# Attention stage of a hybrid block: modulation product in four column groups, a new spread of the maxima, first scores begun early

## The reference, cut to what matters

```python
def one_block(qi):
    s = jnp.einsum('bqhgd,bkhd->bhgqk', qi.astype(F32), k.astype(F32))
    p = jax.nn.softmax(s, axis=-1)
    return jnp.einsum('bhgqk,bkhd->bqhgd', p, v.astype(F32))
...
mod = jax.nn.silu(cond) @ ada_w + ada_b          # 2 condition rows, 1024 x 6144 weights
```

## Time and profile before

| | us |
|---|---|
| median of 3 runs | 3956.98 |
| the profiled execution | 3956.98 |
| its span | 3955.5 |
| around the span | 1.5 |
| attention stage, about | 357 to 1291 |

### The profile page before, as it was taken

One profiled execution on the slowest core, in us unless ns is written; L12 is line 12 of the kernel. 1 busy time (PEld: TensorE's weight loads), 2 busy tenths in 40 slices (PEclk: granted clock), 3 DMA queues, 4 the chain that ended last, 5 costly groups with the idle time before them and its releaser, 6 DMA issues. The chain is left out here.

```text
span 3955.5 us, 51421 instructions
## 1 busy us (share of the span) xinstructions
PE 3598.2 (91%) x17154; PEld 2926.8 (74%) x17154; DVE 1975.2 (50%) x2945; ACT 1587.8 (40%) x2216; POOL 1050.2 (27%) x606
## 2 busy tenths in 40 slices
PE   5886999999998799787869979999999999999998
PEld 2674666666666799666758768888888888888897
DVE  2765888888886211144753333334334333433364
ACT  2443787777887211265223422222222222222233
POOL 0553888888887000011211100000000000000000
PEclk8997999999999899766989989999999999999999
DMA  4332111110110322133544553334334333533374
GB/s 164 105 111 81 38 42 43 39 42 18 43 42 19 120 81 81 61 97 97 157 153 163 170 164 99 113 98 148 97 112 145 98 102 101 154 95 101 101 207 149
DMA packets 374897, 400.59 MB, mean 101 GB/s; under 512 B 37236, under 2 KB 282196, under 8 KB 374772
## 3 DMA queue, kind: packets, MB, share of 16 engines
q1 hardware_dynamic: 358568, 358.26, 29.2%
q0 software_dynamic: 8432, 31.46, 2.1%
q10 hardware_dynamic: 7776, 9.44, 0.7%
HBM read 318.02 MB, written 81.08 MB: 101 GB/s over the span
## 5 line engine op out<-in xcount | busy, mean ns | idle before, releaser
L796 POOL TENSOR_TENSOR att_tlo<-att_prob,att_thi 128x1024 fp32r<-128x1024 f32 x292 | 694.6, 2397 | 152.1 <-ACT att_thi L963 152.1
L331 PE MATMUL ff_p<-ff_hhi,ff_whi 128*128 128x512 f32 (+1 forms) x1760 | 651.2, 370 | 34.3 <-DVE ff_hlo L2038 22.8
L1982 ACT ACTIVATE ff_whi<-ff_ws 128x2048 fp32r<-128x2048 f32 (+1 forms) x170 | 317.5, 1868 | 902.9 <-PE ff_p L333 885.1
L332 PE MATMUL ff_p<-ff_hlo,ff_whi 128*128 128x512 f32 (+1 forms) x1760 | 650.3, 369 | 0.0
L333 PE MATMUL ff_p<-ff_hhi,ff_wlo 128*128 128x512 f32 (+1 forms) x1760 | 650.3, 369 | 0.0
L1986 DVE TENSOR_TENSOR ff_wlo<-ff_ws,ff_whi 128x2048 fp32r<-128x2048 f32 (+1 forms) x170 | 378.4, 2226 | 386.7 <-ACT ff_whi L1982 386.4
L1928 POOL TENSOR_TENSOR ff_rs<-ff_ms,neg_half 128x1 f32<-128x1 f32 x18 | 9.9, 553 | 1595.1 <-DVE ff_ms L2058 1595.1
L331 PEld LDWEIGHTS ff_p<-ff_hhi,ff_whi 128*128 128x128 f32 x1760 | 334.2, 190 | 91.8 <-issue 36.7
L958 ACT ACTIVATE att_prob<-att_p_s 128x512 f32<-128x512 f32 x584 | 338.3, 595 | 151.3 <-PE att_p_s L856 127.1
L1002 DVE TENSOR_REDUCE att_mx<-att_p_r 128x1 f32<-128x512 f32 x512 | 343.4, 683 | 76.2 <-PE att_p_r L820 76.2
L333 PEld LDWEIGHTS ff_p<-ff_hhi,ff_wlo 128*128 128x128 f32 x1760 | 334.3, 190 | 55.3
(11 more groups left out here) (239 smaller groups left out, 6264.3 us busy)
## 6 DMA issues: line engine op xcount, KB each, us to landing
ff_ws<-in_w_ffn_dram SPq DMA_DIRECT2D x320, 512.0 KB, 4.8
att_aw<-in_ada_w_dram SPq DMA_DIRECT2D x8, 2048.0 KB, 8.3
proj_d<-gp_out SPq DMA_DIRECT2D x18, 784.0 KB, 4.0
hT_d<-qkv_hT SPq DMA_DIRECT2D x18, 512.0 KB, 2.8
qT_d<-qkv_qT SPq DMA_DIRECT2D x18, 512.0 KB, 2.9
att_qa<-qT_d SPq DMA_DIRECT2D x36, 256.0 KB, 2.8
gp_h<-hT_d SPq DMA_DIRECT2D x18, 512.0 KB, 4.9
qkT_d<-gs_qkT SPq DMA_DIRECT2D x18, 512.0 KB, 3.6
```

The costliest lines, as they stand in the source:

```text
L331: pe.matmul(out, ah, bh, start=first, stop=False)
L332: pe.matmul(out, ah, bl, start=False, stop=False)
L796: pool.tensor_tensor(tlo[:, sl, :], prob[:, sl, :], thi[:, sl, :].bitcast(F32), ALU.subtract).then_inc(s.lo, 1)
L1982: act.activation(whi[:, par, 0:cols], ws[:, par, 0:cols], ACT.Copy).then_inc(s.w_hi, 1)
```

## The change

1. `PLAN` becomes 3, 3, 2, 2, 2, 2, 2, 2, 0: the same 18 pieces, more of them in steps 0 and 1, fewer in 3 and 5.
2. The modulation product of a half chunk is made in one step (step 5, at its end) and in four column groups: the two condition rows are padded to 32 stationary columns (`cpad`, made once at the start of the stage), and four products of 64 columns go to the output partitions 0, 32, 64 and 96. That is 8 x 4 matmuls of 64 columns in place of 8 of 256, in one visit in place of four. The bias addition moves to step 6, on 128 partitions x 64; the bias load and the store take the new layout (4 partitions per condition row, two stores in place of one), and SyncE waits for `cpad` before it loads the first chunk.
3. In step 0 of a latent unit, the high parts of both first scores are begun at once, and only their low parts wait for the copy of the maxima; these now stand after the first piece, one behind the other.

```diff
@@ -589,7 +589,7 @@
     FULL = T_LAT // ROW
     N_PIECES = G4 * FULL + G4 // 2
 
-    PLAN = [2, 2, 2, 3, 2, 3, 2, 2, 0]
+    PLAN = [3, 3, 2, 2, 2, 2, 2, 2, 0]
     FOLDED = (2, 6)
     BANKS = 3
     ADDS = 2 * NS - len(FOLDED)
@@ -597,15 +597,17 @@
 
     CHUNKS = N_MOD * D_MODEL // 512 - MOD_FIRST
     HALF = 256
-    CHUNK_STEP = 4
+    CHUNK_STEP = 5
+    COLS = P // 4
+    QUART = HALF // 4
     L_UNITS = 2 * N_LAT
     U_UNITS = 2 * NT
     with ExitStack() as stack:
         ph = Phase(nc, stack, "att")
         s = ph.s
...
         s.q, s.out = [s.q0, s.q1, s.q2, s.q3], [s.out0, s.out1]
         ckr = ph.sb("ckr", [P, 2, KVH, HD])
         cvr = ph.sb("cvr", [P, 2, KVH, HD])
@@ -626,8 +628,9 @@
         osum = ph.sb("osum", [P, 2, P])
         oo = ph.sb("oo", [P, 2, 2 * P])
         aw = ph.sb("aw", [P, KC, 512])
-        adab = ph.sb("adab", [2, 512])
-        mod = ph.sb("mod", [2, 512])
+        cpad = ph.sb("cpad", [P, KC, COLS])
+        adab = ph.sb("adab", [P, 2, QUART])
+        mod = ph.sb("mod", [P, 2, QUART])
         ada_w = g.ada_w.rearrange("l (k p) n -> p (l k) n", p=P)
         p_s = [ph.ps(f"p_s{i}") for i in range(BANKS)]
         p_r = [ph.ps("p_r0"), ph.ps("p_r1")]
@@ -760,8 +763,9 @@
                     cols = bass.ds(c * 512 + MOD_FIRST * 512, 512)
                     sp.dma_start(aw[:, :, :], ada_w[:, :, cols]).then_inc(s.aw, 16)
                     for r in range(2):
-                        sp.dma_start(adab[r:r + 1, :], g.ada_b[:, cols]).then_inc(s.adab, 16)
-
+                        sp.dma_start(adab[r:P:COLS, :, :], g.ada_b[:, cols].rearrange("o (h q n) -> (o q) h n", h=2, q=4)).then_inc(s.adab, 16)
+
+                sp.wait_ge(s.cpad, 1)
                 load_chunk(0)
 
                 def step(S):
@@ -773,13 +777,15 @@
                     if S.after is not None and S.after[1] == 1:
                         c = S.after[0]
                         sp.wait_ge(s.mod, c * 2 + 2)
-                        sp.dma_start(g.mod_d[:, bass.ds(c * 512 + MOD_FIRST * 512, 512)], mod[:, :]).then_inc(s.mout, 16)
+                        for r in range(2):
+                            sp.dma_start(g.mod_d[r:r + 1, bass.ds(c * 512 + MOD_FIRST * 512, 512)].rearrange("o (h q n) -> (o q) h n", h=2, q=4),
+                                         mod[r:P:COLS, :, :]).then_inc(s.mout, 16)
                         if not (isinstance(c, int) and c == CHUNKS - 1):
-                            sp.wait_ge(s.mout, c * 16 + 16)
+                            sp.wait_ge(s.mout, c * 32 + 32)
                             load_chunk(c + 1)
 
                 schedule(sp, step)
-                sp.wait_ge(s.mout, 16 * CHUNKS)
+                sp.wait_ge(s.mout, 32 * CHUNKS)
 
             @block.gpsimd
             def _(pool):
@@ -843,17 +849,21 @@
                         turn(*S.turn)
                     pieces = list(S.max)
 
-                    def scores(i):
+                    def key_cols(e, j, i):
+                        return slice((e.kt0 + 2 * j + i) * P, (e.kt0 + 2 * j + i + 1) * P)
+
+                    def scores_high(i):
                         e, j = S.now
-                        half = (e.g0 + j) * 2 + i
+                        if j == 0 and i == 0:
+                            pe.wait_ge(s.q[e.q], e.q_round * 32 + 32)
+                        wait(pe, s.ex, (e.g0 + j) * 2 + i - (BANKS - 1))
+                        pe.matmul(bank_of(e, j, i)[:, :], g.keysT[:, e.kv, 0, key_cols(e, j, i)], qa[:, e.q, :], start=True, stop=False)
+
+                    def scores_rest(i):
+                        e, j = S.now
                         if j == 0 and i == 0:
                             pe.wait_ge(s.aux, e.n + 1)
-                            pe.wait_ge(s.q[e.q], e.q_round * 32 + 32)
-                        wait(pe, s.ex, half - (BANKS - 1))
-                        bank = bank_of(e, j, i)
-                        kt = slice((e.kt0 + 2 * j + i) * P, (e.kt0 + 2 * j + i + 1) * P)
-                        pe.matmul(bank[:, :], g.keysT[:, e.kv, 0, kt], qa[:, e.q, :], start=True, stop=False)
-                        pe.matmul(bank[:, :], g.keysT[:, e.kv, 1, kt], qb[:, e.q, :], start=False, stop=True).then_inc(s.st, 1)
+                        pe.matmul(bank_of(e, j, i)[:, :], g.keysT[:, e.kv, 1, key_cols(e, j, i)], qb[:, e.q, :], start=False, stop=True).then_inc(s.st, 1)
 
                     def values(i):
                         b, j = S.val
@@ -871,8 +881,13 @@
                         if i == 1:
                             last.then_inc(s.pv, 1)
 
+                    first = bool(late and S.now[1] == 0)
                     if S.now:
-                        scores(0)
+                        scores_high(0)
+                        if first:
+                            scores_high(1)
+                        else:
+                            scores_rest(0)
                     if S.turn and late:
                         turn(*S.turn)
                     if S.turn_sums:
@@ -893,24 +908,30 @@
                         values(0)
                     if pieces:
                         piece(*pieces.pop(0))
-                    if S.now:
-                        scores(1)
+                    if first:
+                        scores_rest(0)
+                        scores_rest(1)
+                    elif S.now:
+                        scores_high(1)
+                        scores_rest(1)
                     if len(pieces) > 1:
                         piece(*pieces.pop(0))
                     if S.val:
                         values(1)
                     for p in pieces:
                         piece(*p)
-                    if S.chunk is not None and CHUNK_STEP <= S.now[1] < CHUNK_STEP + KC // 2:
+                    if S.chunk is not None and S.now[1] == CHUNK_STEP:
 
                         (e, j), (c, half) = S.now, S.chunk
-                        if j == CHUNK_STEP:
-                            wait(pe, s.osum, e.n)
-                            pe.wait_ge(s.aw, c * 16 + 16)
-                        for k in range(2 * (j - CHUNK_STEP), 2 * (j - CHUNK_STEP) + 2):
-                            last = pe.matmul(p_o[1 - e.kv][0:2, 0:HALF], g.cT[:, k::KC], aw[:, k, half * HALF:(half + 1) * HALF], start=k == 0, stop=k == KC - 1)
-                        if j == CHUNK_STEP + KC // 2 - 1:
-                            last.then_inc(s.chunk, 1)
+                        wait(pe, s.osum, e.n)
+                        pe.wait_ge(s.aw, c * 16 + 16)
+                        pe.wait_ge(s.cpad, 1)
+                        for k in range(KC):
+                            for q in range(4):
+                                col = half * HALF + q * QUART
+                                last = pe.matmul(p_o[1 - e.kv][q * COLS:(q + 1) * COLS, 0:QUART], cpad[:, k, :], aw[:, k, col:col + QUART],
+                                                 start=k == 0, stop=k == KC - 1)
+                        last.then_inc(s.chunk, 1)
 
                 schedule(pe, step)
 
@@ -974,6 +995,10 @@
             @block.vector
             def _(dve):
                 dve.memset(ones[:, :], 1.0)
+                dve.memset(adab[:, :, :], 0.0)
+                dve.memset(cpad[:, :, :], 0.0).then_inc(s.zero, 1)
+                dve.wait_ge(s.zero, 1)
+                dve.tensor_copy(cpad[:, :, 0:2], g.cT[:, :].rearrange("p (c k) -> p k c", c=2)).then_inc(s.cpad, 1)
                 dve.memset(wm[:, :, :, :].bitcast(F32), 0.0).then_inc(s.zero, 1)
                 for t in range(2):
                     constant_parts(dve, ckp[:, t])
@@ -990,7 +1015,7 @@
                     dve.tensor_tensor(v_here[:, :, HD:2 * HD], cvr[:, t], v_here[:, :, 0:HD].bitcast(F32), ALU.subtract)
                     last = dve.tensor_tensor(ckp[:, t, :, 2, :], ckr[:, t], ckp[:, t, :, 0, :].bitcast(F32), ALU.subtract)
                 last.then_inc(s.ckl, 1)
-                dve.wait_ge(s.zero, 1)
+                dve.wait_ge(s.zero, 2)
 
                 def piece(v, i, item):
                     bank = item[0]
@@ -1061,12 +1086,11 @@
                                 piece(*pieces.pop(0))
                     for p in pieces:
                         piece(*p)
-                    if S.chunk is not None and S.now[1] == CHUNK_STEP + KC // 2:
+                    if S.chunk is not None and S.now[1] == CHUNK_STEP + 1:
                         e, (c, half) = S.now[0], S.chunk
-                        cols = slice(half * HALF, (half + 1) * HALF)
                         dve.wait_ge(s.chunk, c * 2 + (half + 1))
                         dve.wait_ge(s.adab, c * 32 + 32)
-                        dve.tensor_tensor(mod[:, cols], p_o[1 - e.kv][0:2, 0:HALF], adab[:, cols], ALU.add).then_inc(s.mod, 1)
+                        dve.tensor_tensor(mod[:, half, :], p_o[1 - e.kv][:, 0:QUART], adab[:, half, :], ALU.add).then_inc(s.mod, 1)
 
                 schedule(dve, step)
```

(4 more changed lines are left out.)

## The result

The changed kernel takes 3976.89 us in the median (3974.11 to 3981.11), the kernel before beside it 3957.98 us; ratio 1.0048, 95% interval 1.0035 to 1.0061. It is slower by 19 us, where the forecast was 8.6 us faster. The profiled execution took 3974.11 us, span 3972.2.

A forecast was written before the change was run, and what follows sets the result against it. TensorE was taken to bound product units, GpSimd's chain the second half of plain ones; 16 product units x (0.6 - 1.7) = -17.6 and 15 plain x 0.6 = +9.0 took 3957.0 to 3948.4 us, range 3920 to 3985.

The forecast's parts named there:

- point 5: Padding set-up, smaller bias addition in step 6, second store and SyncE's queued loads: all taken as 0.
- Point 1: Modulation product on TensorE: four visits of 1.15 us, 4.6 us per product unit, become one visit of X.
- X: Time of the product's one visit, 64 passes: 2.2 us taken, between a lower end of 1.4 and 7.7.
- Point 2: Second half of a product unit, L883 to the turn: 10.5 + X, 12.7 us, 1.7 less.
- Point 3: Plan of the maxima: first half 0.6 us longer in both kinds of unit; plain turn wait about 2.1.
- Point 4: Early first scores in step 0: 0.3 us hidden by GpSimd, taken as 0; uncovered 0.3 x 31 = 9 us.
- Rival B: TensorE's clock falls to half speed after half the plain turns: 8 x 1.5 = +12, 3960 us; chance 0.22.
- A: The forecast itself, the sum of the points: 3948.4 us, own range 3938 to 3956; chance 0.35.
- rival C: Product's column groups do not run side by side: X = 3.9, 3976 us, dearer cases 4003 and 4036; chance 0.23.

The follow-up runs named there:

- e13_after_oldplan: The changed kernel with only the old plan of the maxima (2, 2, 2, 3, 2, 3, 2, 2, 0), load not held: 3954.64 us, ratio 0.9991.
- e4_hold_oldplan: The changed kernel with the 2 MB load held past VectorE's jump back and the old plan of the maxima: 3931.31 us, ratio 0.9938.
- e1_hold: The changed kernel, SyncE holding the next 2 MB modulation load until the next unit's step 0 and 1 scores are made: 3950.72 us, ratio 0.9984.
- e8_slices: The changed kernel with the load held and the four product slices side by side in one column group: 3989.26 us, ratio 1.0088.
- e15_bias_held: The changed kernel with only the two small bias loads held, the 2 MB of weights issued as before: 3978.76 us, ratio 1.0051.
- e16_weights_held: The changed kernel with only the 2 MB of weights held, the two bias loads issued in their place: 3951.28 us, ratio 0.9984.

## Why the prediction was wrong

The steps of its sum, one by one:

- **The step that failed is point 5**, "The rest": "its loads for later units queue behind them, for units two ahead. All 0." I looked at what is queued behind SyncE's transfers on its own queue, and never at when the 2 MB load of the next chunk would be issued, though the addition that releases it moved from step 8 to step 6. Step 3 is the place of the store and the load in SyncE's program, not their time: SyncE waits there for nothing but the addition, so in the kernel before the store went out at 552.81, 1.4 us behind the turn, and not in step 3. Moved forward with the addition, the load was issued 0.75 us ahead of the end of VectorE's branch, and the fetch of VectorE's next instructions, which the sum does not have, stood behind it. Price: 23 us (e13_after_oldplan against e4_hold_oldplan) to 26 us (the changed kernel against e1_hold). The kernel before had the sign of it, an idle time "issue" of 14.3 us in six places, longest 2.5, and I did not read that row.
- **Point 1, X, was mis-sized**: 2.2 taken, 1.22 measured. The lower end, 1.4, was the right reading: all four groups side by side. The row of two first weight loads, 0.06 apart, said nothing about loads in a stream: 64 passes with a load each start 0.014 us apart. Size: 16 x 1.0 = 16 us too dear. The page "TensorE: Matmul & The Clock Gate" of the Trainium skill, section "The mechanism", says that a load overlaps matmuls in flight only where the row group differs (the same section also lets a load into the background weight buffer be pulled ahead). The trace disagrees with the "only", as it did for the whole array: these loads all use all rows, and even in one column group (e8_slices) passes start 0.056 us apart with a load of 0.11 us before each, which is what streaming alone asks.
- **Point 2** was right as 10.5 + X. A product unit's second half is 26.55 - 14.62 = 11.9 us, and 10.5 + 1.22 = 11.7. That the turn would wait about 1 us there was right as well (0.93).
- **Point 3** was right: first half 14.62 in both kinds of unit (13.97 + 0.6 was said), L898 waits up to 1.0, the turn up to 2.0 (2.1 was said), plain units 26.4 (26.3). The fin waits 0.3 for its bank (0.25). It missed the six units that begin an iteration: with the load held they take 27.5 us against 26.2 before, 1.4 more where the sum has 0.6.
- **Point 4** was right for this change, where L898's wait hides the early scores. With the old plan they cost 0.3 us a unit, the uncovered price that the point names.
- **Rival B was true beside A.** I had them as alternatives, and they are two terms of one sum. After turns of nearly 2 us in plain units the clock is granted at half in some of the product units that follow. The windows of TensorE's clock there (granted clock in the third column from the end), and the timeline of the turn:

```profile
515.10:518.50 3.40, 3.40 (x10) 2.62 (x9) 1.40 (x2) 2.23 (x3) 1.68 (x1) 0.50 0.12 30
518.50:520.20 1.70, 1.70 (x9) 1.37 (x8) 0.90 (x2) 0.54 (x3) 1.60 (x1) 1.00 0.50 171
```

```profile
514.49 0.65 PE L841 MATMUL att_p_r<-ident,att_wm 128*128 128x128 f32 x4 [1.98 <-DVE att_wm L1035]
...
515.74 0.63 PE L860 MATMUL att_p_s<-att_qa,keysT 128*128 128x512 f32 x1
...
518.63 0.40 PE L880 MATMUL att_p_o<-att_tlo,vals 128*128 128x512 f32 x1
```

TensorE idled 1.98 us, ran from 515.1 to 518.5 at 1.2 GHz with 0.63 us a matmul, and then at 2.4 GHz with 0.40. Such a unit takes 28.11 in place of 26.55 us: 1.56, where B had 1.5. There are six in the changed kernel, 9 us (B: eight, 12 us), and more behind the long stalls.

With what was measured the sum comes near: forecast -8.6, X -16, clock +14 (nine units in e1_hold) gives -11, the first units of an iteration add 4.6 more than it had, and e1_hold, the change without the stall, stands at -6 us against the kernel before. That its 3950.7 lies so near the 3948.4 forecast is luck: X was too dear, the clock and the first units were left out, and the errors cancel. With the stall on top it is the result. The range, to 3985, held the time only by luck too: its upper end came from rival C, and the column groups do run side by side.

The Trainium skill has the reason for a fetch at all, in "Runtime: NRT & Kernel Launch", section "Instruction fetch mechanics": a taken branch to a target outside the pages held forces a DMA fetch before execution goes on. The 2.7 us at the branch agree with it in kind, and the packet of an instruction queue in each stall does too. That the fetch can stand behind a kernel's own load is shown here by the start of that packet, and by e1_hold, e15_bias_held and e16_weights_held.

Open: why the fetch gets its turn when a little over half of the 2 MB have gone ahead of it, and what decides in which units the clock falls, since the waits ahead of those that kept it were as long.

## What to carry to other kernels

When an edit moves a result to an earlier step, follow it to every transfer that it releases, and set the new issue time of the large ones against the jump back of each engine's loop (it was VectorE's that counted here; the others were not looked at); a wait named "issue" that recurs once an iteration is the place to look. A small wait on a step that is sure to come after the jump (one line here) was worth 26 us. And slack ahead of a turn can be filled with work that only has to be done some time: moving the product's visit to step 7 brought 11.6 us.

## What the runs showed of the hardware

A 2 MB load issued 0.75 us ahead of VectorE's jump back lengthens its stall from 2.75 to 6.0 us; 512 KB make it 3.9 to 4.6; a load issued 0.8 us behind the jump leaves it at 2.75. The fetch's packet starts 0.9 to 1.0 us after the branch in the kernel before and 3.9 to 4.3 us after it behind the 2 MB load, and VectorE goes on 1.8 to 2.0 us after that start in both. Sixty-four float32 passes of 64 columns, each with its own weight load of 32 columns (106 to 110 ns by the record), start within 0.88 us on four column groups and within 3.54 us on one.
